# Expert weights stored in DRAM piece by piece, one transfer with rows of 16 KB for each piece

## The chip, the cores and the metric

The kernel is one program on 1 core of one Trainium2 chip. The metric is device microseconds (us) of one execution; shorter is better. All data are float32.

## The reference

One decoder layer over 1024 tokens of width 1024: an attention sub-layer with a sliding window of 128, and then a mixture of experts, both with an RMSNorm that the conditioning vector shifts, scales and gates, and a last RMSNorm. What matters here is the mixture: each token goes to 4 of 32 experts.

```python
def _moe(h, w_r, b_r, w_in, b_in, w_out, b_out):
    ...
    logits = hf @ w_r + b_r
    top_val, top_idx = lax.top_k(logits, TOP_K)
    gates = jax.nn.softmax(top_val.astype(jnp.float32), axis=-1).astype(h.dtype)
    ...
    def expert_block(args):
        xb, e = args
        u = xb @ w_in[e] + b_in[e]
        return _clamped_swiglu(u) @ w_out[e] + b_out[e]
```

`w_in[e]` is 1024 x 2048 (8 MB), `w_out[e]` is 1024 x 1024 (4 MB), so the weights of one expert are 12 MB and those of all 32 are 403 million bytes.

## The kernel before

**Stages.** The first 570 us hold the modulation vectors, the attention and, token tile by token tile, the router. Then the tokens are brought to the experts. POOL scatters each token's number into the list of each of its experts, a table `list_d` in DRAM (L483; 32 scatters of 128 numbers of 4 bytes, the last four for the last token tile). When all are in (L485), it reads the lists back (L490), TensorE puts them in the order of the experts (L1310, L1311), and POOL gathers the rows of the first expert from `xn_d` in DRAM (`gather_rows`, L492 to L497: 128 rows of 4 KB, and for a wide expert a second gather with the rest). TensorE transposes the rows (L1326), and the work on the first expert begins.

**Slots.** The experts are taken in 32 slots in the order of their token counts. The table `WIDTHS` gives each slot its number of columns: 192, 184 and so on down to 144 for the first twelve, and 128 for the other twenty. In a slot TensorE makes 128 products for `w_in` (L1347; 8 steps of 16) and 64 for `w_out` (L1379; 8 steps of 8), between them the transposes of the last slot's result (L1338) and of the next slot's rows (L1326). POOL gathers the rows of the next slot when the transposes of this slot's rows are done, and stores the result of the last one (`store_rows`, L504). After slot 31 POOL gathers each token's four results (L523), and the last norm and the store follow.

**Weights.** A ring of six pieces of 2 MB in SBUF, one row of 4096 floats in each of 128 partitions, holds exactly one expert: pieces 0 to 3 are `w_in`, pieces 4 and 5 `w_out`. SP loads them, each when TensorE has made the last step that reads its former content. These lines set the order; `steps_to` counts the steps of the slot before:

```python
        steps_to = [2, 4, 6, 8, 12, 16]
...
            sp.wait_ge(s_row, 1)
            for r in range(E):
                e = sp.value_load(experts[:, r:r + 1], min_val=0, max_val=E - 1)
                for p in range(NPIECE):
                    if r:
                        sp.wait_ge(s_mm, (r - 1) * 16 + steps_to[p])
                    load_piece(sp, e, p, s_wl[p])
```

For slot 0 there is nothing to wait for but the number of the expert (`s_row`, written by L938), so all six pieces are asked for at once, while the lists are still being made. `load_piece` (L311 to L320) cuts a piece out of the weights as they come: for `w_in` two transfers of 1 MB (L316), each 128 partitions by 8 runs of 256 floats, 1 KB; for `w_out` one of 2 MB (L320) with 8 runs of 512 floats, 2 KB, in each partition. A transfer's end adds 16 to the piece's semaphore, and TensorE waits at L1353 and L1370 for the sums in `PIECE_DONE` (L322). An overflow branch for experts with more tokens than their width, which uses the same `load_piece`, stands behind the stages above; it is not entered with these inputs.

Of the kernel before, what the change touches and what calls it, by code (L numbers as in the profile page):

```python
# [19 lines left out]
P = 128  # L20
D = 1024
SEQ = 1024
KT = D // P
# [5 lines left out]
E = 32  # L29
# [11 lines left out]
PIECE = 4096  # L41
NPIECE = 6
# [17 lines left out]
def program(nc, x, c, w_mod, vecs, w_qkv, w_o, sinks, rel_table, router_w, router_b,  # L60
# [9 lines left out]
    with ctx:  # L70
# [19 lines left out]
        def piece(p):  # L90
            return ring[:, p * PIECE:(p + 1) * PIECE]
# [132 lines left out]
        def bank(b, n=1):  # L224
            return ps[:, 512 * b:512 * (b + n)]
# [79 lines left out]
        def head_at(place):  # L305
            return 2 * (place % 2) + place // 2

        w_in_v = moe_w_in.rearrange("e (k p) (s q n) -> e q p k s n", p=P, s=2, n=256)
        w_out_v = moe_w_out.rearrange("e (k p) (q n) -> e q p k n", p=P, n=512)

        def load_piece(eng, e, p, done):  # L311

            if p < 4:
                dst = piece(p).rearrange("p (k s n) -> p k s n", k=KT, s=2)
                for s in range(2):
                    eng.dma_start(dst[:, :, s, :], w_in_v[bass.ds(e, 1), p, :, :, s, :].rearrange("o p k n -> (o p) k n"))\  # L316
                        .then_inc(done, 16)
            else:
                dst = piece(p).rearrange("p (k n) -> p k n", k=KT)
                eng.dma_start(dst, w_out_v[bass.ds(e, 1), p - 4].rearrange("o p k n -> (o p) k n")).then_inc(done, 16)  # L320

        PIECE_DONE = [32, 32, 32, 32, 16, 16]  # L322

        def x_rounds(r):
            return 4 if wide(r) else 2
# [13 lines left out]
        def _(sp):  # L339
# [68 lines left out]
# [6 lines that stand above are left out]
# [11 lines left out]
            with sp.If(n_more >= 1):  # L425
                with sp.Fori(0, NOVER) as i:
                    with sp.If(i < n_more):
                        slot = sp.value_load(over_slot[:, bass.ds(i, 1)], min_val=0, max_val=E - 1)
                        e = sp.value_load(experts[:, bass.ds(slot, 1)], min_val=0, max_val=E - 1)
                        sp.wait_ge(s_ofree, i * 1 + 1)  # L430
                        for p in range(NPIECE):
                            load_piece(sp, e, p, s_ow)
                store_out(TT)
# [301 lines left out]
        def _(dve):  # L735
# [62 lines left out]
            for n, (kind, t, _) in enumerate(groups):  # L798
                if kind == "v":
                    dve.wait_ge(s_qkv, n + 1)  # L800
                    dve.tensor_tensor(out=vv[:, t, :], in0=bank(n % 4)[:, 0:256], in1=bvB[:, :], op=ALU.add)\  # L801
                        .then_inc(s_qv, 1)
                for piece_n in mod_after.get(n, ()):
                    mod_evacuate(piece_n)
                    if piece_n + 2 < NMOD:
                        mod_sum_of(piece_n + 2)
# [313 lines left out]
        def _(pe):  # L1120
# [20 lines left out]
            for t in range(TT):  # L1141
                pe.wait_ge(s_xn, t + 1)
                for h in range(2):
                    n = 2 * t + h
# [197 lines left out]
            def slot(r):  # L1342
# [8 lines left out]
                for j in range(8):  # L1351
                    if j % 2 == 0:
                        pe.wait_ge(s_wl[j // 2], (r + 1) * PIECE_DONE[j // 2])  # L1353
                    if j >= 4:
# [13 lines left out]
                for m in range(8):  # L1368
                    if m % 4 == 0:
                        pe.wait_ge(s_wl[4 + m // 4], (r + 1) * PIECE_DONE[4])  # L1370
                    if m < 4:
# [22 lines left out]
            with pe.If(n_more >= 1):  # L1394
                pe.wait_ge(s_acc, TT)
                pe.sem_inc(s_ofree, 1)
                with pe.Fori(0, NOVER) as i:
                    with pe.If(i < n_more):
                        pe.wait_ge(s_og, i * 16 + 16)
                        for k in range(KT):  # L1400
                            last = pe.transpose(bank(4 + k // 4)[:, k % 4 * P:(k % 4 + 1) * P], xg[:, 0, k * P:(k + 1) * P],
                                                ident[:, :])
                        last.then_inc(s_ox, 1)
                        pe.wait_ge(s_oxT, i * 1 + 1)
                        pe.wait_ge(s_ow, i * 160 + 160)
                        for j in range(8):
                            w = piece(j // 2).rearrange("p (k s n) -> p k s n", k=KT, s=2)
                            if j >= 4:
                                pe.wait_ge(s_oact, i * 8 + j - 3)
                            for s in range(2):  # L1410
                                for k in range(KT):
                                    last = pe.matmul(bank(j % 4)[:, s * 256:s * 256 + P], w[:, k, s, (j % 2) * P:(j % 2 + 1) * P],
                                                     xT[:, k, 0:P], start=(k == 0), stop=(k == KT - 1))
                            last.then_inc(s_omm, 1)
                        pe.wait_ge(s_oact, i * 8 + 8)
                        for m in range(8):
                            if m >= 4:
                                pe.wait_ge(s_ome, i * 8 + m - 3)
                            w = piece(4 + m // 4).rearrange("p (k n) -> p k n", k=KT)
                            for k in range(KT):  # L1420
                                last = pe.matmul(bank(m % 4)[:, 0:P], w[:, k, (m % 4) * P:(m % 4 + 1) * P], actT[:, k, 0:P],
                                                 start=(k == 0), stop=(k == KT - 1))
                            last.then_inc(s_omm, 1)
                        pe.wait_ge(s_ome, i * 8 + 8)
                        for h in range(2):
                            for m in range(4 * h, 4 * h + 4):
                                last = pe.transpose(bank(6 + h)[:, (m % 4) * P:(m % 4 + 1) * P], yT[:, m, 0:P], ident[:, :])
                            last.then_inc(s_oyt, 1)
                        pe.wait_ge(s_oye, i * 2 + 2)
                        pe.wait_ge(s_oyst, i * 16 + 16)  # L1430
                        pe.sem_inc(s_ofree, 1)
# [51 lines left out]
```

## Time and profile before

| | |
|---|---|
| median of 3 runs | 2300.09 us (2298.84 to 2300.12) |
| the profiled execution | 2298.75 us, its span 2296.9 us |
| TensorE (PE) busy | 2094.3 us, 91% |
| VectorE, ScalarE, GpSimd busy | 30%, 21%, 8% |
| DRAM read, written | 481.34 MB, 30.23 MB |
| DMA packets | 377299 |
| mean rate over the span | 223 GB/s |

The profiled execution took 2298.75 us, of which 2296.9 us lie between the first and the last instruction. The DMA packets are the contiguous runs of the transfers. SP's queue (q1) carries the weights, POOL's (q0) the scatters, gathers and result stores, ScalarE's (q10) seven small loads at the start.

### The profile page before, as it was taken

The page shows a single profiled execution, that of the slowest core. Times are in us where ns is not written, and L with a number is a line of the kernel's source. Part 1 is how long each engine was busy: PE and PEld are TensorE (multiplying, and loading weights), DVE is VectorE, ACT ScalarE, POOL GpSimd, SP SyncE. Part 2 cuts the span into 40 slices and gives each one's busy share as a digit, 9 for nine tenths or more (in the row PEclk, how much of TensorE's full clock was granted, in tenths as well). Part 3 has the DMA queues.
Part 4 walks back from the last instruction along what each step waited for, and adds up shares of the span by engine and source line. Part 5 has one row for each costly group of instructions (what it writes and reads, how often), then busy time and mean ns, then how long its engine had stood idle before and what let it go on. Part 6 is the DMA issues. An engine that isn't in the chain of part 4 may idle for free.

```text
span 2296.9 us, 35824 instructions
## 1 busy us (share of the span) xinstructions
PE 2094.3 (91%) x15349; PEld 1927.2 (84%) x15349; DVE 690.7 (30%) x1786; ACT 478.0 (21%) x1310; POOL 186.4 (8%) x225
## 2 busy tenths in 40 slices
PE   3958999997599999999999999999999999999950
PEld 2634886665599999999999999999999999999950
DVE  5722554553132222212222222212212221221227
ACT  4101443442111111111111111211121121112111
POOL 2002100113100000000000000000000000000025
PEclk9979999997599999999999999999999999999985
DMA  9850001001966666677777889999998999999836
GB/s 346 246 129 20 5 34 47 28 19 36 247 204 225 220 232 222 231 243 244 256 257 255 277 287 312 311 307 303 306 315 293 311 312 308 303 304 315 277 121 258
DMA packets 377299, 514.98 MB, mean 224 GB/s; under 512 B 10878, under 2 KB 277522, under 8 KB 377106
## 3 DMA queue, kind: packets, MB, share of 16 engines
q1 hardware_dynamic: 359202, 458.23, 61.4%
q0 software_dynamic: 16336, 54.05, 6.4%
q8 instruction: 123, 2.02, 0.4%
q10 hardware_dynamic: 1600, 0.36, 0.1%
q14 instruction: 38, 0.31, 0.1%
HBM read 481.34 MB, written 30.23 MB: 223 GB/s over the span
## 4 chain that ended last, share of the span: by engine, by line
PE 86%; DMA 3%; issue 3%; POOL 3%; DVE 2%; SPq 2%; ACT 1%; POOLq 0%; ACTq 0%; DVEq 0%
PE ps L1347 43%; PE ps L1379 21%; PE ps L1236 5%; PE ps L1165 4%; PE ps L1326 2%; PE ps L1243 2%; PE ps L1209 2%; PE ps L1338 2%; POOL ring L523 2%; PE ps L1184 1%; SPq L376 1%; PE ps L1196 1%; DMA U<-in_w_mod 1%; DMA list_d<-tok_i,dest 1%; DMA xr<-in_x 1%
## 5 line engine op out<-in xcount | busy, mean ns | idle before, releaser
L1347 PE MATMUL ps<-U,ring 128*128 128x128 f32 (+7 forms) x8192 | 1012.1, 286 | 1.0 <-ACT U L679 1.0
L1347 PEld LDWEIGHTS ps<-U,ring 128*128 128x128 f32 x8192 | 1005.7, 192 | 1.3 <-ACT U L679 1.2
L1379 PE MATMUL ps<-U,ring 128*128 128x128 f32 (+7 forms) x4096 | 512.3, 286 | 0.0
L1379 PEld LDWEIGHTS ps<-U,ring 128*128 128x128 f32 x4096 | 501.9, 191 | 1.7 <-DVE U L1020 0.2
L1011 DVE TENSOR_SCALAR U<-ps,U 128x128 f32<-128x128 f32 (+7 forms) x256 | 93.3, 364 | 1231.1 <-PE ps L1347 1231.0
L687 ACT ACTIVATE U<-U 128x128 f32<-128x128 f32 (+7 forms) x256 | 82.2, 321 | 964.6 <-DVE U L1011 964.6
L694 ACT ACTIVATE U<-ps,U,modT 128x128 f32<-128x128 f32 (+7 forms) x256 | 120.9, 472 | 332.9 <-PE ps L1379 332.9
L1236 PE MATMUL ps<-ring 128*128 128x512 f32 x256 | 116.8, 610 | 3.1 <-DVE xr L868 2.6
L1165 PE MATMUL ps<-ring 128*128 128x512 f32 x192 | 88.3, 620 | 25.8 <-DVE U L801 24.1
L495 POOL DMA_INDIRECT U<-xn_d,U x44 | 44.5, 1012 | 754.0 <-PE ps L1326 743.0
L679 ACT ACTIVATE U<-ps,modT,Af 128x128 f32<-128x128 f32 (+7 forms) x256 | 99.4, 472 | 30.4 <-PE ps L1326 30.3
L1236 PEld LDWEIGHTS ps<-ring 128*128 128x128 f32 x256 | 48.4, 194 | 63.1 <-issue 62.3
L1165 PEld LDWEIGHTS ps<-ring 128*128 128x128 f32 x192 | 37.7, 199 | 72.2 <-issue 47.7
L1013 DVE TENSOR_SCALAR U<-ps,U 128x128 f32<-128x128 f32 (+7 forms) x256 | 91.0, 355 | 0.0
L504 POOL DMA_DIRECT2D y_d<-U x44 | 24.9, 567 | 800.2 <-DVE U L1004 800.2
L1020 DVE SCALAR_TENSOR_TENSOR U<-U 128x128 f32<-128x128 f32 (+7 forms) x256 | 78.4, 306 | 8.9
L1018 DVE TENSOR_TENSOR U<-U 128x128 f32<-128x128 f32 (+7 forms) x256 | 75.4, 294 | 0.0
L1326 PE MATMUL ps<-ident,U 128*128 128x128 f32 x352 | 65.2, 281 | 9.9 <-DMA U<-xn_d,U 9.9
L1326 PEld LDWEIGHTS ps<-ident,U 128*128 128x128 f32 x352 | 45.1, 140 | 28.1 <-issue 18.3
L631 ACT ACTIVATE ring<-ring,negm 128x256 f32<-128x256 f32 (+1 forms) x128 | 61.4, 483 | 21.8 <-DVE dsk L838 21.8
L1243 PE MATMUL ps<-ring 128*128 128x256 f32 x256 | 61.7, 395 | 2.2 <-ACT U L661 2.1
L1243 PEld LDWEIGHTS ps<-ring 128*128 128x128 f32 x256 | 48.8, 196 | 13.8 <-issue 3.9
(200 smaller groups left out, 1234.0 us busy)
## 6 DMA issues: line engine op xcount, KB each, us to landing
ring<-in_moe_w_in SPq DMA_DIRECT2D x256, 1024.0 KB, 7.7
ring<-in_moe_w_out SPq DMA_DIRECT2D x64, 2048.0 KB, 8.0
U<-in_w_mod SPq DMA_DIRECT2D x8, 2048.0 KB, 20.1
y_d<-U POOLq DMA_DIRECT2D x32, 512.0 KB, 6.9
ring<-in_w_mod SPq DMA_DIRECT2D x4, 2048.0 KB, 18.4
ring<-in_w_qkv SPq DMA_DIRECT2D x3, 2048.0 KB, 18.3
xr<-in_x SPq DMA_DIRECT2D x8, 512.0 KB, 13.3
ring<-in_w_o SPq DMA_DIRECT2D x2, 2048.0 KB, 7.9
```

Of the source, the lines that this page charges most:

```text
L679: last = act.activation(xT[:, k, 0:n], bank(4 + q % 2)[:, at:at + n], ACT.Identity, scale=Af[:, k:k + 1], bias=modT[:, 24 + k:25 + k])
L687: act.activation(sbuf_[:, j % 2, 0:n], gbuf[:, j % 2, 0:n], ACT.Sigmoid, scale=1.702)\
L694: act.activation(yT[:, m, 0:n], bank(m % 4)[:, 0:n], ACT.Identity, scale=modT[:, 40 + m:41 + m], bias=biasT[:, 16 + m, r:r + 1]).then_inc( ...
L1011: dve.tensor_scalar(gbuf[:, j % 2, 0:n], bank(j % 4)[:, 0:n], biasT[:, j, r:r + 1], 7.0, ALU.add, ALU.min).then_inc(s_gr, 1)
L1013: dve.tensor_scalar(lbuf[j % 3][:, 0:n], bank(j % 4)[:, 256:256 + n], biasT[:, 8 + j, r:r + 1], -6.0, ALU.add, ALU.max).then_inc(s_je, 1)
L1020: dve.scalar_tensor_tensor(out=actT[:, j, 0:n], in0=lbuf[j % 3][:, 0:n], scalar=8.0, in1=gsbuf[:, j % 2, 0:n], op0=ALU.min, op1=ALU.mult). ...
L1165: last = pe.matmul(bank(n % 4), w[:, k, m * P:(m + 1) * P], hT[:, k, h * 512:h * 512 + 512], start=(k == 0), stop=(k == KT - 1))
L1236: last = pe.matmul(bank(7), attnT[:, k, t * P:(t + 1) * P], wo[:, k, h * 512:h * 512 + 512], start=(k == 0), stop=(k == KT - 1))
L1243: last = pe.matmul(bank(7)[:, 0:256], wq[:, k, m * P:(m + 1) * P], hT[:, k, 512 + z * 256:768 + z * 256], start=(k == 0), stop=(k == KT - 1))
L1326: last = pe.transpose(bank(4 + q % 2)[:, at:at + rows], xg[0:rows, b, k * P:(k + 1) * P], ident[0:rows, 0:rows])
L1347: return pe.matmul(bank(j % 4)[:, s * 256:s * 256 + n], w[:, k, s, (j % 2) * P:(j % 2 + 1) * P], xT[:, k, 0:n], start=(k == 0), stop=(k == ...
L1379: last = pe.matmul(bank(m % 4)[:, 0:n], w[:, k, (m % 4) * P:(m % 4 + 1) * P], actT[:, k, 0:n], start=(k == 0), stop=(k == KT - 1))
```

## The change

The host stores `moe_w_in` as 32 x 4 x 128 x 4096 and `moe_w_out` as 32 x 2 x 128 x 4096 floats, in the order in which the pieces lie in SBUF. `load_piece` issues one transfer for each piece, 128 rows of 16 KB. Its semaphore counts follow. What lies in SBUF, what TensorE computes and the order of the pieces stay as they are.

```diff
-        w_in_v = moe_w_in.rearrange("e (k p) (s q n) -> e q p k s n", p=P, s=2, n=256)
-        w_out_v = moe_w_out.rearrange("e (k p) (q n) -> e q p k n", p=P, n=512)
-
         def load_piece(eng, e, p, done):
 
-            if p < 4:
-                dst = piece(p).rearrange("p (k s n) -> p k s n", k=KT, s=2)
-                for s in range(2):
-                    eng.dma_start(dst[:, :, s, :], w_in_v[bass.ds(e, 1), p, :, :, s, :].rearrange("o p k n -> (o p) k n"))\
-                        .then_inc(done, 16)
-            else:
-                dst = piece(p).rearrange("p (k n) -> p k n", k=KT)
-                eng.dma_start(dst, w_out_v[bass.ds(e, 1), p - 4].rearrange("o p k n -> (o p) k n")).then_inc(done, 16)
-
-        PIECE_DONE = [32, 32, 32, 32, 16, 16]
+            src = moe_w_in[bass.ds(e, 1), p] if p < 4 else moe_w_out[bass.ds(e, 1), p - 4]
+            eng.dma_start(piece(p), src.rearrange("o p n -> (o p) n")).then_inc(done, 16)
+
+        PIECE_DONE = [16] * NPIECE
...
-                        pe.wait_ge(s_ow, i * 160 + 160)
+                        pe.wait_ge(s_ow, i * 96 + 96)
...
-        "moe_w_in": np.asarray(moe_w_in)[0],
+        "moe_w_in": np.asarray(moe_w_in)[0].reshape(E, KT, P, 2, 4, 256).transpose(0, 4, 2, 1, 3, 5).reshape(E, 4, P, PIECE),
...
-        "moe_w_out": np.asarray(moe_w_out)[0], "final_g": np.asarray(final_norm_g),
+        "moe_w_out": np.asarray(moe_w_out)[0].reshape(E, KT, P, 2, 512).transpose(0, 3, 2, 1, 4).reshape(E, 2, P, PIECE), "final_g": np.asarray(final_norm_g),
```

Only SP's instructions differ. This is how they stand at the beginning of the weights of slot 0, before; `vecr` holds the expert numbers, and each `ISA` computes an address:

```order
L409 TENSOR_LOAD vecr [waits expert_row_ready]
L409 ISA x2
L316 ISA
L316 DMA ring<-in_moe_w_in 128x8x256
L316 ISA
L316 DMA ring<-in_moe_w_in 128x8x256
L316 ISA
L316 DMA ring<-in_moe_w_in 128x8x256
L316 ISA
L316 DMA ring<-in_moe_w_in 128x8x256
```

and now (the file is nine lines shorter at this place, so L409 is L400, and L316 is L311):

```order
L400 TENSOR_LOAD vecr [waits expert_row_ready]
L400 ISA x2
L311 ISA
L311 DMA ring<-in_moe_w_in 128x4096
L311 ISA
L311 DMA ring<-in_moe_w_in 128x4096
L311 ISA
L311 DMA ring<-in_moe_w_in 128x4096
L311 ISA
L311 DMA ring<-in_moe_w_in 128x4096
```

The four DMAs shown load pieces 0 and 1 before, and pieces 0 to 3 now. At slot 1, where the waits for TensorE's steps (`step_product`) begin, SP had these rows:

```order
L409 TENSOR_LOAD vecr
L409 ISA x2
L316 ISA [waits step_product]
L316 DMA ring<-in_moe_w_in 128x8x256
L316 ISA
L316 DMA ring<-in_moe_w_in 128x8x256
L316 ISA [waits step_product]
```

and has these:

```order
L400 TENSOR_LOAD vecr
L400 ISA x2
L311 ISA [waits step_product]
L311 DMA ring<-in_moe_w_in 128x4096
L311 ISA [waits step_product]
```

Each piece has the wait that it had, with one DMA behind it in place of two.

## Rows read from the trace of the kernel before

**Rows 1.** The page: TensorE's granted clock and the DMA engines in 40 slices
```profile
PEclk9979999997599999999999999999999999999985
DMA  9850001001966666677777889999998999999836
```

**Rows 2.** Waits of TensorE from 617 to 2217 us: total, times, longest
```profile
PE ps L1347 <- ACT U L679: 1.0, 1, 1.0
PE ps L1338 <- ACT U L694: 0.6, 1, 0.6
```

**Rows 3.** Stretches: us, busy (x count) of PE, PEld, DVE, ACT, POOL, clock, DMA, GB/s
```profile
617.00:2181.00 1564.00, 1563.92 (x12678) 1545.93 (x12679) 350.61 (x1103) 289.32 (x748) 66.27 (x85) 1.00 0.83 275
2181.00:2199.00 18.00, 18.00 (x164) 18.00 (x163) 5.50 (x20) 1.55 (x5) 0.00 (x0) 1.00 0.08 30
```

**Rows 4.** Groups by line, 1400 to 1445 us: busy us, mean ns of one, idle before
```profile
L1347 PE MATMUL ps<-U,ring 128*128 128x128 f32 x256 | 28.9, 275 | 0.0
```

**Rows 5.** The same groups from 2181 to 2199 us
```profile
L1347 PE MATMUL ps<-U,ring 128*128 128x128 f32 x164 | 18.5, 275 | 0.0
```

**Rows 6.** The chain of waits from 560 to 625 us: start us, us, what
```profile
575.85 17.16 DMA list_d<-tok_i,dest
593.01 0.29 issue
593.30 5.97 DMA U<-list_d
...
601.22 1.02 POOL U L495
602.24 0.30 issue
602.54 7.75 DMA U<-xn_d,U
610.29 0.14 issue
610.43 5.66 PE ps L1326 x16
616.09 0.02 issue
616.11 0.92 ACT U L679 x2
617.03 0.04 issue
617.08 8.03 PE ps L1347 x33
```

**Rows 7.** SP's queue from 540 to 640 us: start us, us, what
```profile
575.12 31.98 SPq L316 DMA_DIRECT2D ring<-in_moe_w_in  x8
607.29 7.54 SPq L320 DMA_DIRECT2D ring<-in_moe_w_out  x2
```

**Rows 8.** Stretches around the start of slot 0, columns as in rows 3
```profile
560.00:576.00 16.00, 8.98 (x41) 8.08 (x41) 5.38 (x33) 2.90 (x8) 11.60 (x13) 0.50 0.03 1
576.00:588.00 12.00, 9.82 (x49) 9.12 (x49) 2.82 (x19) 0.05 (x1) 0.81 (x1) 0.50 0.91 44
588.00:593.00 5.00, 0.00 (x0) 0.00 (x0) 0.00 (x0) 0.18 (x1) 0.00 (x0) 0.50 1.05 284
593.00:610.00 17.00, 0.98 (x4) 0.78 (x4) 2.25 (x9) 0.00 (x0) 2.50 (x3) 0.50 1.05 312
620.00:622.00 2.00, 2.00 (x8) 2.00 (x7) 0.00 (x0) 0.00 (x0) 0.00 (x0) 0.50 1.05 397
```

**Rows 9.** DMA issues from 1500 to 2170 us: KB each, median us to landing
```profile
y_d<-U POOLq DMA_DIRECT2D x15, 512.0 KB, 7.0
U<-xn_d,U POOLq DMA_INDIRECT x14, 7.8
```

**Rows 10.** DMA issues from 2181 us on
```profile
y_d<-U POOLq DMA_DIRECT2D x1, 512.0 KB, 3.3
```

**Rows 11.** ScalarE's last two loads at the start: issue, us, what
```profile
3.51 0.49 ACTq L574 DMA_DIRECT2D brB<-in_router_b  x1
4.03 3.24 ACTq L575 DMA_DIRECT2D wr<-in_router_w  x1
```

**Rows 12.** The page, DMA issues: KB each, us to landing
```profile
wr<-in_router_w ACTq DMA_DIRECT2D x1, 128.0 KB, 17.7
brB<-in_router_b ACTq DMA_DIRECT2D x1, 16.0 KB, 11.7
```

## The prediction

> **What bounds the kernel now.** I read the page's slices first. The DMA engines are at nine tenths for the last third of the expert stage [rows 1], which invites the thought that the weights bound it. The next view, the waits of TensorE, says otherwise: from 617 to 2217 us it waits 1.6 us in all, both times for ScalarE and never for a piece of weights [rows 2]. The stretches agree: of the 1564 us from 617 to 2181 TensorE is busy 1563.92 [rows 3]. So the slots are a solid row of products, and weights that come sooner are weights that lie in SBUF longer.
>
> One more way for DMA to matter there would be that its writes slow the products. The groups by line answer it. A product of 128 columns takes 275 ns on average while the weights stream at about 300 GB/s [rows 4], and 275 ns when the stream has ended and 30 GB/s are left [rows 3, 5]. So that costs nothing now and gives nothing back.
>
> What is left is the one place where the path to the end runs through DMA while weights are under way: the start of slot 0. The chain of waits shows it [rows 6]. POOL issues the last scatter at 575.85; it lands 17.16 us later. The lists are read back in 5.97 us, two small products order them, two gathers are issued at 601.22 and 602.54, and the second lands after 7.75 us, at 610.29. Transposes follow, and at 617.08 the products begin. SP issues the weights of slot 0 at 575.12, 0.7 us before that last scatter, and is still issuing at 614.8 [rows 7]. So all four small transfers of this chain share the 16 DMA engines with the stream of weights, and the change alters the packets of just that stream.
>
> **The change, part by part.**
>
> *Fewer instructions on SP.* 128 transfers of 320 go, at four a slot. SP's issues only took time because its queue was full: eight took 31.98 us [rows 7]. Nobody waits for SP's issues but through the pieces, and no wait for a piece shows [rows 2]. Worth 0. The new thing is that SP has all six pieces of slot 0 in its queue within about 3 us (six issues at the 0.4 to 0.7 us that an issue takes when the queue is free, the nearest being ScalarE's 0.49 [rows 11]). The stream then has no gap until its 12.6 MB are in.
>
> *Faster stream in slots 1 to 31.* Hidden behind TensorE in full [rows 2, 3]: 0. What could come from it is a loss, if a gather or a result store (7.8 and 7.0 us now [rows 9]) became so slow that a slot waits for it. Each has most of a slot, about 44 us for the narrow ones, since the gathers run one slot ahead; even 10 us more are covered. 0, with both ends at 0.
>
> *The end of the kernel.* No weights are in flight there [rows 3]: 0.
>
> *The start of slot 0.* Here I need to know how POOL's queue and SP's share an engine. Two readings.
> First, how long a small transfer waits for its turn. A store of 512 KB lands 3.3 us after issue when nothing else runs [rows 10], and 7.0 us in the stream of weights [rows 9]. So it waits 3.7 us, in which a stream of about 312 GB/s [rows 8] moves 1.15 MB, 72 KB on each engine: with 1 KB packets that is some 70 packets. Either bytes or packets could be what is counted.
> Second, whether it then goes through in one piece. ScalarE's last two loads at the start tell. `brB` lands at 3.51 + 11.7 = 15.2 us and `wr`, right behind it on the same queue, at 4.03 + 17.7 = 21.7 [rows 11, 12]. `wr` is 128 KB in runs of 128 bytes, 1024 packets, 64 on each engine. It took 6.5 us, 0.10 us for each of its packets, far too long for 128 bytes. SP's stream had packets of 2 KB then, and 2 KB on each of 16 engines at some 340 GB/s last 0.097 us. So I read that the queues take turns **packet by packet**: one small packet, one of the stream's.
>
> With 16 KB packets each such turn costs more. At 380 GB/s (I take a value between 312 and 397 [rows 8], nearer the upper, since longer runs should help) 16 KB on each of 16 engines last 262 KB / 380 GB/s = 0.69 us, against 16.4 KB / 312 GB/s = 0.05 us for 1 KB. The price of each step of the chain:
> - Gathers: slot 0 has 192 rows, 8 and then 4 on each engine. 12 x (0.69 - 0.05) = **+7.7 us**. The stream does not run out first: 0.5 MB are in at 588 (12 us at 44 GB/s [rows 8]), and the other 12.1 MB at 380 GB/s last until about 620, while the gathers would land near 618.
> - List read: 2 rows on each engine, which count as one or two turns: +0.7 us, between 0.6 and 1.3.
> - Last scatter: one turn for its data, one for its completion: +0.7 us.
> - Turns counted in bytes: the same 72 KB wait at a stream of 380 in place of 312 GB/s is shorter by 0.6 us, for two transfers: -1.2 us.
> - The crawl: from 576 to 588 the stream itself gets only 44 GB/s though the engines are 0.91 busy [rows 8], right behind sixteen scatters in a row, whose 4-byte writes I take to hold up DRAM. The last scatter stands in the queue behind it. Whether rows of 16 KB crawl more or less no row shows. Bounds: if the wait grows by as much as one more MB at 284 GB/s [rows 8], +4 us; if the crawl goes and the scatter lands 4 us after its issue, as the free store does [rows 10], -13 us. I take 0: what drains there are the scatters' own writes, and they are the same.
>
> Sum: 7.7 + 0.7 + 0.7 - 1.2 = +7.9 us, 2298.75 + 7.9 = 2306.7 for the profiled execution, which is 1.3 us below the median. I give **2307 us**. TensorE is at half clock until about 622 in either case, since it idles before; the rise should move with the first transposes.
>
> The Trainium skill, "DMA: Bandwidth & Descriptors", section on queues, rings and completion order, says that an engine drains a whole packet of several descriptors, typically 9 to 17, from one queue before it turns to the next. That would be turns by whole transfers here, the second rival. The same page's table of bandwidth puts large transfers near 425 GB/s; at that value, an estimate, the gathers' term would be 6.8 us.
>
> **Rivals.**
> 1. *Nothing happens.* A queue's turn counts bytes, also within a row of 16 KB, so a small transfer sees the same stream as before. For it: the 3.7 us fit a count of bytes. Against: `wr`'s 0.10 us. Then only the -1.2 us and noise are left: 2299 to 2301. Chance 0.28.
> 2. *Whole transfers take turns.* A small transfer waits for at most one transfer on each engine: now 1 MB, 3.4 us at 312 GB/s, then 2 MB, 5.5 us at 380, and then goes through at once. Three waits in a row grow by up to 2.1 us, +4 at a likely two thirds: 2304. For it: the 3.7 us are about one transfer of 1 MB. Against: a wait that depends on where in a transfer one arrives should scatter, and `wr` would pass in 1 us. Chance 0.12.
> 3. *The stream is queued in packets, not bytes.* If some 70 packets stand ahead, that is all 48 rows that an engine has for slot 0: the scatter waits until about 620, 27 us later. List read and gathers then run free and win back some 3 and 4 us: +20, 2320. Chance 0.06.
> 4. *Faster.* The crawl is what the runs of 1 KB at a pitch of 8 KB do beside the scatters, and rows of 16 KB escape it. The scatter then lands near 580 in place of 593, -13; the gathers still pay the turns, +7.7: about -6, 2294. It decides as soon as the scatter lands before 585. For it: the crawl is strange, and 17.16 us are five times a free landing. Against: `w_in`'s later transfers have the same runs and pitch and move at 284 GB/s and more [rows 8], so the scatters, which stay, are the likelier cause. Chance 0.09.
>
> The forecast keeps 0.45.
>
> **How the numbers follow.** A measurement of this kernel tells 0.2%, 4.6 us, from no change. Slower by that: most of the forecast's 0.45, rival 3 and a part of rival 2, 0.50. Within: rival 1, most of rival 2 and the low end of the forecast, 0.39. Faster: rival 4 and a little of the unknown, 0.11. The range leaves out rivals 3 and 4 and takes in rival 1 and the forecast with its crawl bound of +4: 2297 to 2314.
>
> **What would show it.** In the page: packets down from 377299 to near 72 thousand (24.6 thousand rows of 16 KB in place of 262.1 thousand runs of 1 KB and 65.5 of 2 KB, and 16 completions less for each of 128 transfers), and the DMA digits of the late slices lower for the same GB/s. In the waits of TensorE: still none for pieces, and nearly the whole difference before the first L1347. In the chain: the second gather lands near 15 us after its issue rather than 7.75, the scatter near 17, the list read near 6.5. The forecast is wrong if the gathers land as now (rival 1), if the scatter lands after 40 us (rival 3) or in under 9 (rival 4), or if products in mid-stage take other than 275 ns.

## The result and the profile after

The change makes the kernel slower by 0.3%: 2306.25 us (median of 13 runs, 2304.06 to 2308.32) against 2300.09 (13 runs, 2296.27 to 2300.94), ratio 1.0032, 95% interval 1.0025 to 1.0039. The span of the profiled execution is 2303.9 us against 2296.9, 7.0 more. In the code of the change `load_piece`'s transfer is L311, the scatter L474, the gather L486; the up product is L1338.

The page, the lines that answer to [rows 1], the packets and the weights' transfers (line, engine, op, count, KB each, us to landing):

```profile
PEclk9979999997599999999999999999999999999985
DMA  9850011001855666666677788888888888888736
...
DMA packets 72144, 514.94 MB, mean 224 GB/s; under 512 B 8830, under 2 KB 13330, under 8 KB 47378
...
ring<-in_moe_w_in SPq DMA_DIRECT2D x128, 2048.0 KB, 8.6
ring<-in_moe_w_out SPq DMA_DIRECT2D x64, 2048.0 KB, 7.9
```

The change did what it says: packets fell from 377299 to 72144, and the late slices show 8 where they showed 9. The DMA engines have room to spare, and nothing waits for it. TensorE's waits from 625 to 2225 us, its products from 1400 to 1445 us, and the first stretch of the expert stage, against [rows 2, 4, 3]:

```profile
PE ps L1338 <- ACT U L670: 1.0, 1, 1.0
PE ps L1329 <- ACT U L685: 0.5, 1, 0.5
```

```profile
L1338 PE MATMUL ps<-U,ring 128*128 128x128 f32 x262 | 29.7, 275 | 0.0
```

```profile
625.00:2189.00 1564.00, 1563.76 (x12684) 1545.85 (x12685) 351.01 (x1104) 289.02 (x748) 66.50 (x85) 1.00 0.75 273
```

The DMA share of the stretch fell from 0.83 to 0.75 at nearly the same rate (275 and 273 GB/s), and TensorE is as full as before. The time is in the chain at the start of slot 0, against [rows 6]:

```profile
576.13 18.09 DMA list_d<-tok_i,dest
594.22 0.29 issue
594.51 6.07 DMA U<-list_d
...
603.85 14.59 DMA U<-xn_d,U
618.45 0.14 issue
618.58 5.66 PE ps L1317 x16
...
625.24 14.91 PE ps L1338 x80
```

The second gather takes 14.59 us from issue to landing in place of 7.75, the scatter 18.09 in place of 17.16, the list read 6.07 in place of 5.97: 6.84 + 0.93 + 0.10 = 7.87 us. Of the three only the gather's share is tied to the change by the experiments below; the scatter's time varies by more than this among the traces (12.85 to 18.09 us), and not with the length of the rows. The chain began 0.28 us later, and the products start at 625.24 in place of 617.08. A little comes back behind that, in part by the clock. The stretches in which the granted clock rises, before (first) and after:

```profile
621.00:623.00 2.00, 2.00 (x11) 2.00 (x11) 0.00 (x0) 0.00 (x0) 0.00 (x0) 0.75 1.02 395
```

```profile
628.00:630.00 2.00, 2.00 (x12) 2.00 (x11) 0.00 (x0) 0.00 (x0) 0.00 (x0) 0.85 0.42 133
```

A mean of 0.75 puts the step from half to full at 622.0 us, 4.9 us after the first product; 0.85 puts it at 628.6, 3.4 us after it. From the first product to the issue of the last result store (2216.91 before, 2224.32 after) pass 1599.1 us in place of 1599.8, and that store lands in 2.89 us in place of 3.29. 8.16 - 0.75 - 0.40 = 7.0, the difference of the spans.

SP's queue from 540 to 640 us, against [rows 7], and the stretches of [rows 8] after:

```profile
575.40 2.87 SPq L311 DMA_DIRECT2D ring<-in_moe_w_in  x4
578.47 1.36 SPq L311 DMA_DIRECT2D ring<-in_moe_w_out  x2
```

```profile
576.00:588.00 12.00, 10.10 (x51) 9.40 (x50) 2.94 (x20) 0.00 (x0) 0.96 (x1) 0.50 1.01 81
...
593.00:610.00 17.00, 0.98 (x4) 0.78 (x4) 2.25 (x9) 0.00 (x0) 2.50 (x3) 0.50 0.97 376
```

All six pieces are in the queue by 579.8 us, 4.4 us after the first issue, and the stream behind the crawl moves 376 GB/s in place of 312. The crawl is still there, at 81 GB/s in place of 44.

The trace also keeps the start of every DMA packet, and there the turns can be counted. In the change the gathers' 192 rows begin at 606.8 us, 16 of them at a time, one for each DMA engine; the next 16 start 0.77 us later, and so on for five steps. A packet of 16 KB takes 0.62 us. While the first 128 rows start, to 612.8 us, 125 such packets start too. So after each row of the gather one packet of the stream passes.

### The profile page after: what moved, and what is told of

It is laid out like the page before. It is cut to its first block, busy times and chain, and to the rows that moved or that the text cites. A ratio compares the mean times of both kernels' runs of the same rounds, so it can differ in the third digit from the quotient of the medians.

```text
span 2303.9 us, 35440 instructions
## 1 busy us (share of the span) xinstructions
PE 2093.1 (91%) x15349; PEld 1927.6 (84%) x15349; DVE 691.4 (30%) x1786; ACT 477.6 (21%) x1310; POOL 186.6 (8%) x225
## 2 busy tenths in 40 slices
DMA packets 72144, 514.94 MB, mean 224 GB/s; under 512 B 8830, under 2 KB 13330, under 8 KB 47378
## 4 chain that ended last, share of the span: by engine, by line
PE 85%; DMA 4%; issue 3%; POOL 3%; DVE 2%; SPq 2%; ACT 1%; POOLq 0%; ACTq 0%; DVEq 0%
PE ps L1338 43%; PE ps L1370 21%; PE ps L1227 5%; PE ps L1156 4%; PE ps L1234 2%; PE ps L1317 2%; PE ps L1200 2%; PE ps L1329 2%; POOL ring L514 2%; PE ps L1175 1%; SPq L367 1%; DMA U<-in_w_mod 1%; PE ps L1187 1%; DMA list_d<-tok_i,dest 1%; DMA xr<-in_x 1%
## 5 line engine op out<-in xcount | busy, mean ns | idle before, releaser
L1338 PE MATMUL ps<-U,ring 128*128 128x128 f32 (+7 forms) x8192 | 1011.4, 286 | 1.0 <-ACT U L670 1.0
L1338 PEld LDWEIGHTS ps<-U,ring 128*128 128x128 f32 x8192 | 1005.0, 192 | 1.3 <-ACT U L670 1.2
L486 POOL DMA_INDIRECT U<-xn_d,U x44 | 44.6, 1013 | 760.2 <-PE ps L1317 749.0
```

Source lines behind the costliest of these rows:

```text
L1338: return pe.matmul(bank(j % 4)[:, s * 256:s * 256 + n], w[:, k, s, (j % 2) * P:(j % 2 + 1) * P], xT[:, k, 0:n], start=(k == 0), stop=(k == ...
```

## Experiments

Each ran against the kernel before on the same chip. Chips and rounds of runs differ by some us (medians of the kernel before: 2293.68, 2297.12, 2297.01), so each time is read against its own. Each kernel has one trace; the traces of `rows1k`, `rows4k`, `rows8k` and `slot0_4k` are from one chip, those of the other experiments from a second, and the kernel before was traced in none of these rounds.

**How long are the packets, how large the transfers?** Three kernels keep the change's one transfer of 2 MB for each piece, and the host cuts the rows: a piece lies in DRAM as 4096 / RUN blocks of 128 x RUN floats, so that the contiguous runs have 1, 4 or 8 KB.

```diff
-            src = moe_w_in[bass.ds(e, 1), p] if p < 4 else moe_w_out[bass.ds(e, 1), p - 4]
-            eng.dma_start(piece(p), src.rearrange("o p n -> (o p) n")).then_inc(done, 16)
+            w = (moe_w_in if p < 4 else moe_w_out).rearrange("e c q p n -> e c p q n")
+            src = w[bass.ds(e, 1), p if p < 4 else p - 4]
+            eng.dma_start(piece(p).rearrange("p (q n) -> p q n", n=RUN), src.rearrange("o p q n -> (o p) q n")).then_inc(done, 16)
```

Runs of 1 KB (RUN = 256):

> One transfer of 2 MB for each piece as in the change, but in runs of 1 KB as before (the host stores a piece as 16 blocks of 128 x 256 floats). Theory (queues take turns packet by packet, so the size of the stream's packet sets the price): the second gather of slot 0 lands near 7.8 us after its issue as before, products start near 617 us, the time is that of before within 1.5 us. Rival (queues take turns by whole transfers): the transfers are as large as in the change, so the gather lands near 14 us and the time is 5 to 7 us above before.

Runs of 4 KB:

> The same with runs of 4 KB in one transfer of 2 MB. Theory: the gather's delay is linear in the packet, 7.75 us at 1 KB and 14.59 us at 16 KB, so near 9.1 us here, and the time is 1 to 2 us above before. Rival (whole transfers): 14 us, 5 to 7 us above before.

Runs of 8 KB:

> The same with runs of 8 KB. Theory: the gather lands near 10.9 us, the time is 2.5 to 4 us above before. Rival (whole transfers): 14 us, 5 to 7 us above before.

The second gather of slot 0 in the chains of the three, in this order:

```profile
597.55 7.34 DMA U<-xn_d,U
```

```profile
594.78 8.53 DMA U<-xn_d,U
```

```profile
599.63 10.92 DMA U<-xn_d,U
```

The times against before: 1.0001 (0.9992 to 1.0011), 1.0002 (0.9993 to 1.0012), 1.0018 (1.0008 to 1.0027). With 1 KB in a 2 MB transfer nothing is lost, so the size of the transfer is not what costs: turns by whole transfers are out. With the run the gather grows steadily, 7.34, 8.53, 10.92, then 14.59 in the change. The 4 KB kernel's median is nearly that of before, where 1 to 2 us of loss were expected; its interval runs from 1.6 us less to 2.8 us more and holds both. The 8 KB kernel is 4.1 us above before by the ratio, just over the 2.5 to 4 expected.

While the first 128 rows of the gathers start, 130, 134 and 132 packets of the stream start in these three. The turns are the same at every size, one packet for each row, and only the packet's length differs. The kernel before is an exception that I can't explain: there 318 packets of 1 KB start in that time, though its gather lands only 0.41 us later than that of `rows1k`.

One expectation failed. The products of `rows1k` start at 611.67 us and not near 617, since its last scatter lands 13.91 us after its issue. In `rows4k` it is 12.85 and in `rows8k` 14.34, against 17.16 and 18.09 in the kernel before and the change. So the start of the products can't be compared between these traces and the first two, and the scatter's 0.93 us more in the change can't be put down to the change.

**Does the price stay linear?** The pieces lie in pairs in DRAM, and slot 0 alone is loaded in three transfers of 4 MB with rows of 32 KB; later slots load rows of 16 KB out of the pairs.

```diff
...
+                if r == 0:
+                    for h in range(3):
+                        w = (moe_w_in if h < 2 else moe_w_out)[bass.ds(e, 1), h % 2]
+                        sp.dma_start(ring[:, 2 * h * PIECE:2 * h * PIECE + 2 * PIECE], w.rearrange("o p z n -> (o p) (z n)"))\
+                            .then_inc(s_wl[2 * h], 16)
...
```

> The pieces lie in pairs in DRAM, so that slot 0 takes three transfers of 4 MB with rows of 32 KB, while slots 1 to 31 load single pieces in rows of 16 KB as in the change. Theory (one row of the gather, one packet of the stream): the runs at 1, 4, 8 and 16 KB gave 7.3, 8.5, 10.9 and 14.6 us for the second gather, about 0.48 us more for each KB, so 22 us at 32 KB, or less by what remains when the stream ends first, near 620 us; the time is 9 to 15 us above before. Rival (what costs is that SP has the whole slot in the queue at once, not the packet): 14 to 15 us as in the change, 6 us above before. Rival (long rows are cut into packets of 16 KB or less): the same.

Measured: 2310.78 us, ratio 1.0060 (1.0043 to 1.0077), some 14 us above before. Its chain and its count of packets:

```profile
575.22 13.79 DMA list_d<-tok_i,dest
589.01 2.81 issue
591.82 7.43 DMA U<-list_d
...
602.53 21.99 DMA U<-xn_d,U
...
631.30 18.72 PE ps L1342 x105
```

```profile
DMA packets 71712, 514.94 MB, mean 223 GB/s; under 512 B 8782, under 2 KB 13282, under 8 KB 47330
```

22 us were foretold from the slope and 21.99 came. From 7.34 us at 1 KB to 21.99 at 32 KB are 0.47 us for each KB of the stream's packet. Slot 0's 12 rows on each engine give 0.039 us for a row and KB; 1 KB on each of 16 engines lasts 0.044 us at the 376 GB/s of the change from 593 to 610 us and 0.039 at this kernel's 420. So about one packet of the stream passes for each row of the gather, and the packets say the same: 117 of 32 KB start while the first 128 rows do. The packets fell by 432 against the change: 768 rows of 16 KB are now 384 rows of 32 KB, and there are three completions of 16 less, so a row of 32 KB is one packet and isn't cut.

The list read tells that a turn is not a bundle of packets. It has one packet on each engine, and it takes 5.44 us beside packets of 1 KB and 7.43 beside packets of 32 KB. That is 2.0 us more, less than two packets of 1.22 us. One thing in this chain was not expected and stays open: 2.81 us pass between the scatter's landing and the issue of the list read, where the change has 0.29.

**Is all of the loss in slot 0?** The change's layout, but the six pieces of slot 0 go in four transfers each with rows of 4 KB, slots 1 to 31 as in the change.

```diff
...
+                        for q in range(4):
+                            part = slice(q * 1024, q * 1024 + 1024)
+                            sp.dma_start(piece(p)[:, part], w[:, :, part].rearrange("o p n -> (o p) n")).then_inc(s_wl[p], 16)
...
```

> The change's layout, but the six pieces of slot 0 alone are loaded in four transfers each with rows of 4 KB; slots 1 to 31 keep the rows of 16 KB. Theory (all of the loss arises at the start of slot 0): gather near 9.1 us, time 1 to 2 us above before. Rival (rows of 16 KB also cost something in the later slots, by slower gathers, result stores or instruction fetches): the time stays more than 4 us above before though the gather of slot 0 is fast again.

Ratio 0.9991 (0.9982 to 1.0001), no loss where 1 to 2 us were expected; the gather:

```profile
595.34 8.65 DMA U<-xn_d,U
```

The loss is gone with 31 slots still in rows of 16 KB, so the later slots pay nothing for them that shows. The small transfers there are a little slower. DMA issues of the change from 1500 to 2170 us, against [rows 9]:

```profile
y_d<-U POOLq DMA_DIRECT2D x15, 512.0 KB, 7.6
U<-xn_d,U POOLq DMA_INDIRECT x14, 8.2
```

That is 0.6 and 0.4 us more, far less than 8 turns of 0.6. The packets show why: while the 128 rows of one of these 14 gathers start, 31 to 62 packets of 16 KB start, in the median 34, which is two for each engine. SP has little in flight there, so the turns soon end, and nothing waits for these transfers.

**What if the chain has the engines to itself?** SP waits until both gathers of slot 0 have landed; once on the change and once on the kernel before.

```diff
+                    elif p == 0:
+                        sp.wait_ge(s_g, gathers[1] * 16)
                     load_piece(sp, e, p, s_wl[p])
```

> The change, and SP waits until both gathers of slot 0 have landed before it asks for slot 0's first piece, so that the whole chain (scatters, list read, gathers) has the DMA engines to itself. Theory A (the crawl from 576 to 588 us is the scatters' own 4-byte writes draining, as the prediction took it): the last scatter still lands about 12 us after its issue, list read near 3 us, gather near 4, piece 0 about 8 us later; products start near 607 us in place of 625, the time is near 2288. Theory B (the weights' reads make the crawl): the scatter lands about 4 us after its issue, products start near 598, the time is near 2279. Rival to both (the chain only moves the wait to the first piece of weights): products start no earlier than 617, the time is at or above that of before.

On the kernel before:

> The same wait in the kernel before, with its runs of 1 and 2 KB. Once nothing of the chain shares the engines with the weights, the layout should matter only by the time of the first piece: 2 MB in rows of 16 KB against two transfers of 1 MB in runs of 1 KB, about 1 us. Expected: within 2 us of the same wait on the changed layout, likelier above it. Rival (the long rows also cost something elsewhere): it is 3 us or more below.

And a shorter wait, for the last scatter only (`sp.wait_ge(s_sct, TT * TOPK * 16)` in the same place), on the change:

> The change, and SP waits only until the last scatter has landed. The scatter lands as in the longer wait; list read (6 us) and gathers (14.6 us) share the engines with rows of 16 KB again. Theory A: products start near 619 us, time near 2300. Theory B: products start near 611, time near 2292.

The chain with the long wait on the change, and its stretch behind the last scatter:

```profile
574.58 14.14 DMA list_d<-tok_i,dest
589.01 2.10 DMA U<-list_d
...
594.38 4.32 DMA U<-xn_d,U
...
598.88 7.92 DMA ring<-in_moe_w_in
606.94 43.18 PE ps L1340 x255
```

```profile
576.00:588.00 12.00, 8.54 (x43) 7.84 (x43) 2.64 (x16) 0.23 (x1) 0.00 (x0) 0.50 0.01 1
```

This settles the crawl as far as the weights go. The engines are 0.01 busy from 576 to 588 us, the last scatter's packets have all started by 576.3, and still it lands only after 14.14 us. So the weights' reads are not what it waits for. That its own writes and those of the scatters before it drain is what is left, and I read it so. Theory A holds, the products start at 606.94 as it said. In the kernel before and in the change, where the weights are asked for 0.7 us before the last scatter, its packets start only at 590.3 to 591.5 and at 591.2 to 592.5 us, behind the crawling weights, and it lands 1.5 and 1.8 us after them. Without weights the list read takes 2.10 us and the second gather 4.32. The times: 2286.19 us, ratio 0.9948 (0.9931 to 0.9964); the same kernel again in another round 2287.47 us, 0.9965 (0.9950 to 0.9979), by the ratio 8 us below before, where 10 to 12 were expected. On the kernel before the same wait gives 2289.03 us, 0.9967 (0.9954 to 0.9979), 2.8 us above the change with the wait in the same round, a little more than the expected 2. Its TensorE waits 3.4 us for the first piece where the other waits 2.4:

```profile
PE ps L1349 <- DMA ring<-in_moe_w_in: 3.4, 1, 3.4
```

```profile
PE ps L1340 <- DMA ring<-in_moe_w_in: 2.4, 1, 2.4
```

The rest of the 2.8 us I leave open; the two intervals overlap. So with the wait in both, no run shows that the new layout is worth anything.

The short wait was a miss, 2302.55 us, ratio 1.0021 (1.0011 to 1.0031), where 2300 was expected, and its products start at 624.16, where 619 was:

```profile
578.84 13.12 DMA list_d<-tok_i,dest
592.25 6.85 DMA U<-list_d
...
602.37 15.01 DMA U<-xn_d,U
```

In this execution the scatters themselves came 2.7 us later than in the change, and list read and gather pay the turns in full. What a wait has to keep away from is the gathers.

**Can the first piece use the idle time?** From the last scatter's issue to its landing the engines are idle. Here piece 0 goes out once POOL has issued the last scatter, pieces 1 to 5 after the gathers.

```diff
+            pool.engine_nop().then_inc(s_iss, 1)
             pool.wait_ge(s_sct, TT * TOPK * 16)
...
+                    elif p == 0:
+                        sp.wait_ge(s_iss, 1)
+                    elif p == 1:
+                        sp.wait_ge(s_g, gathers[1] * 16)
```

The long wait again, beside it:

> The kernel of hold_gather unchanged, beside the next one on the same chip: 10 to 12 us below before, with TensorE waiting some 2.4 us for its first piece of weights.

> As hold_gather, but the first piece of slot 0 goes out as soon as POOL has issued its last scatter, in the 13 us in which the scatters drain and the engines are idle; pieces 1 to 5 wait for both gathers. Theory (the scatters' packets are already through the engines and only their writes drain, so a single piece behind them costs them nothing): the scatter lands after 14 us as in hold_gather, list read and gathers run free, TensorE does not wait for the first piece, and the time is 2 to 3 us below hold_gather. Rival (the reads of the weights and the scatters' writes slow each other in DRAM): the scatter lands 2 us or more later, and the time is that of hold_gather or above it.

The theory was wrong. The time is 2292.06 us, ratio 0.9977 (0.9967 to 0.9986), above the long wait beside it (2287.47 us) as the rival had it, though the two intervals overlap.

```profile
575.75 15.21 DMA list_d<-tok_i,dest
590.96 0.28 issue
591.25 4.76 DMA U<-list_d
...
599.28 4.74 DMA U<-xn_d,U
```

The list read takes 4.76 us and not 2.01, since the reads of piece 0, which crawl at 52 GB/s from 576 to 588 us, are still going on from 588 to 593 (206 GB/s). That is 2.75 us more, as much as the 2.7 us that TensorE waits for piece 0 in the kernel beside it. The products start 5.0 us later. 2.1 of these are the last scatter's later issue, before the two kernels differ. The scatter lands 15.21 us after it in place of 13.65. That is less than the rival's 2 us, and one piece need not be the reason: in `slot0_32k`, from the same round, the whole of slot 0 is asked for 2 us behind the last scatter, and it lands after 13.79.

## Why the prediction was right

- *The expert stage is bound by TensorE, and a faster stream is worth 0.* Right: DMA share 0.83 to 0.75, the same busy time, 275 ns a product in both. `slot0_4k` shows it by itself.
- *The gathers pay, +7.7 us.* Measured +6.84. The mechanism, turns packet by packet, stands by five sizes of run, by a second trace at 16 KB (15.01 in `hold_scatter`), and by the count of packets, 125 for 128 rows. The term was 0.9 us too large: it took 0.64 us for each row, and the slope gives 0.47 x 15 / 12 = 0.59. The stream's 380 GB/s in it were nearly right (376). The shorter wait for the first turn, booked apart at -1.2 us for two transfers, is contained in what the landing shows. The row that turns were read from, `wr`'s, was read too sharply: the packets of `brB` and `wr` start from 8.97 to 21.14 us and not from 15.2 on, 1152 of them beside 1709 of SP's, of 2 and 4 KB. That is one and a half for each, still turns of a packet or two and not of whole transfers.
- *List read +0.7, scatter +0.7, first turns -1.2: together +0.2.* Measured 0.10 + 0.93 = +1.0. With the gathers it makes 7.87 against 7.9, and that this is so close is luck: the gathers' error is made good by the scatter's 0.93 us, and the scatter takes 12.85 to 14.34 us in the five other traces with weights beside it, with no order by the length of their rows (13.79 at 32 KB). No run shows what a row of 16 KB costs the scatter.
- *The crawl, 0, drained by the scatters' own writes.* Right in that the scatter lands no sooner, and it was a guess between -13 and +4: no row of before could show it. `hold_gather` showed that the wait stays when the weights are away.
- *The clock's rise moves with the first transposes.* The first transposes moved by 8.15 us, the rise by 6.6. TensorE spends 1.5 us less of its products at half clock, which is worth 0.75 us and makes up part of the gap between 7.87 and the span's 7.0.
- *The basis.* The sum gave 2306.7 for the profiled execution, which took 2305.70. I gave 2307 for the median, though median and sum make 2300.09 + 7.9 = 2308.0; it came at 2306.25. The last step was not worked out, and it helped.
- Of the rivals, *nothing happens* falls with the 14.59 us, *whole transfers* with `rows1k`, *queued in packets* with the scatter's 18.09 us beside 48 rows queued: what stands ahead of a small transfer is counted in bytes, or in something that goes with them. The first row of the gathers starts 4.0 to 4.8 us after their issue beside runs of 1 to 32 KB, and 1.7 us without weights. *Faster* needed the scatter before 585 us; it came at 594.22. The rule of the Trainium skill, "DMA: Bandwidth & Descriptors", queues, rings and completion order, that a packet of several descriptors passes before the turn changes, doesn't fit these two queues in these traces: a row of the gather and a packet of the stream alternate, 128 to 125, and the list read at 32 KB is only 2.0 us slower.

## What to carry to other kernels

Before you make a stream's packets longer, look for small transfers on the critical path that run beside it: here each of their rows waited for about one packet of the stream, so long rows raised their price while the stream itself was hidden anyway. Runs of 4 KB cost nothing that could be measured here, and gained nothing. Better still, hold a prefetch back until the short chain that everything waits for is through: with one wait on SP the new layout took 0.35 to 0.52% less than the kernel before, and the old one 0.33% less.

## What was not expected of the hardware

- A scatter of 128 numbers of 4 bytes, the sixteenth in a row at 1.27 us each, lands 13.12 to 14.14 us after its issue with the DMA engines 0.01 to 0.02 busy (the four traces in which the weights wait for it or for the gathers). Its packets start within 2 us; what it waits for shows in no DMA share. I take it for the writes into DRAM, which no run shows by itself.
- Reads beside this wait crawl while the engines look busy: from 576 to 588 us the stream moves 44 and 81 GB/s in the kernel before and the change, and 49 to 201 in the five other kernels that stream there.
- A row of 32 KB goes as one packet, and the linear price held up to there.
